# Two Strassen feed-forwards of a transformer block: modulation turns one place later, two loads earlier, a third set of sums and the last gates in another order

## The chip, the cores and the metric

The kernel runs on one core of one Trainium2 chip. The metric is the time of one execution on the device in microseconds (us). Before the change three runs gave 2195.95, 2199.52 and 2200.91 us; their median is 2199.52 us. Shares and times below are of the core's five engines: PE (TensorE, matmuls), DVE (VectorE), ACT (ScalarE), POOL (GpSimd) and SP (SyncE, which here only issues transfers).

## What is computed

One transformer block on 1024 latent tokens and 256 context tokens of width 1024, in float32. Both token sets pass a first feed-forward, then a token mixer (a bidirectional mLSTM beside banded attention), and the latent tokens pass a second feed-forward. Everything is modulated by vectors that come from a condition `c` through `w_ada`:

```python
mod_l = (jax.nn.silu(c) @ w_ada[l] + b_ada[l]).reshape(B, N_MOD, 1, D)      # nine vectors of 1024
def _ffn_sublayer(x, shift, scale, gate, w13, w2, g, b):
    h = x * (1.0 + scale) + shift
    a = h @ w13                                   # 1024 x 5632
    y = (silu(a[..., :2816]) * a[..., 2816:]) @ w2   # 2816 x 1024
    return _layer_norm(ALPHA * x + FFN_RES * gate * y, g, b)
```

## The kernel before

Each float32 operand is split into a rounded high part (ACT copies it) and a low part (DVE subtracts), and PE multiplies high by high, high by low and low by high. So every operand costs one ACT and one DVE instruction, and every 128-row tile three matmuls.

**First phases** (`quick1_*` for the first feed-forward F1, `quick2_*` for the second, F2). The products with `w13` run by Strassen's scheme in the form with seven products. There are 20 *starts* j, one for each block of 128 hidden columns beyond the first two. In a start PE runs seven products of 12 matmuls (`PRODUCTS`, i = 0 to 6), in F1 with four short products for the context rows between them. DVE adds products together (L1093: `u_sum`, twice `v_sum`, `x_c_sum`, `g_half`), makes the sums of the weights of the next start (L957 to L962) and their low parts (L990). PE's sixth product (i = 5) waits for the third of the L1093 sums, the second `v_sum`. The raw weights of the start after that are loaded when the low parts of `A12` and `A22` have been taken (`quick_weights`).

In F1's first phase DVE also works out the other seven modulation vectors. They come in 112 *slices* of `w_ada`, loaded one by one; DVE multiplies each into `ada_sums` (L741). For the first three vectors each slice is used twice, for latent and context. There are 20 such *units* (`MOD_UNITS`). When a unit is complete PE turns it by four small transposes (L757), and DVE reduces it and adds a bias (L766, L767). `mods_turned(j, place)` says in which of four places of a start a unit is turned. For PE the places are: before product i = 3, before i = 4, before i = 6, and before i = 1 of the next start. For DVE they are: after the low parts of S2 and S1, after the low part of S3, after the context gate (L1103), and after the first two low parts of the next start.

**Second phases** (`second1_*`, `last_*`). The products with `w2` run by Strassen too: seven products of 11 *pieces* each, 77 steps s, 12 matmuls each (L1483 to L1485). A piece is 128x1024: a half from the hidden rows, which the first phase has written to `f_terms`, and a half of `w2`. Six raw buffers (`RAWS`) hold pieces; ACT makes the high part (L1431), DVE the low part (L1470). The weights of products q = 1 to 4 are sums of two halves of `w2`, so another half, `s_kept`, is loaded for each of the 11 pairs, and DVE adds it to the raw piece (L1466). In step s DVE first does the sum of step s + 2 and then the low part of step s, in its own order.

SP issues everything in one queue in program order, and each issue waits for what frees its buffer. Pieces 0 to 3 are issued at the beginning of the last start, pieces 4 and 5 when the first phase's last product is done, and the others when the low part of the piece six before has been taken. The kept halves are issued one by one behind pieces 5 to 15, and each waits until the kept half two before it has landed:

```python
def kept_sp(sp, S, i):
    if i >= 2:
        sp.wait_ge(S.kept_in[i % 2], S.kept_before + 16 * (i // 2))
    sp.dma_start(S.kept[:, i], w2_view[...]).then_inc(S.kept_in[i % 2], 16)
```

The hidden rows of the last pair of blocks are also summed by DVE (`term_rest_dve`: L479, L481, L484) and stored by SP; the three sums come before the low part of piece 2.

**The end.** The last nine steps of the 77 (`TAIL`) run row tile by row tile: t = 0 goes through all nine pieces, then t = 1, 2 and 3. DVE multiplies each finished PSUM tile by the gate (L1540, `gate_part_dve`), adds it to the residual (L1549, `add_part_dve`), and norms the output rows (L3305, L3309, `out_rows_dve`). ACT takes the row sums of all rows but the last (`row_sums_act`), POOL the power (L3252). For the last row DVE does the statistics itself (L3286 to L3293).

## Time and profile before

| | |
|---|---|
| three runs | 2195.95, 2199.52, 2200.91 us |
| span of the profiled execution, first to last instruction | 2195.6 us |
| own time of the profiled execution | not given beside its span; the span is 0.35 us under the shortest run and 3.9 us under the median |
| PE busy | 2152.4 us, 98% |
| DVE busy | 1518.4 us, 69% |
| ACT busy | 890.3 us, 41% |
| DMA, mean over the span | 141 GB/s |
| F1: first phase with `quick1`, second phase | about 109 to 625 us, 625 to 900 us |
| F2: first phase with `quick2`, second phase | about 1590 to 1970 us, 1970 to 2185 us |

A matmul of 512 columns is shown as 0.39 us long, but in an unbroken run one starts every 0.2265 us, so the records overlap; a gap between records is therefore shorter than the time that PE lost. What is lost is read from the distances between starts. Three matmuls of one row tile take 0.68 us, one step of 12 takes 2.72 us.

### The profile page before, as it was taken

How to read it: one execution, taken by the hardware profiler on the slowest of the kernel's cores; microseconds unless marked ns; L12 is line 12 of the kernel's file. 1: busy time of each engine (PE TensorE's matmuls, PEld its weight loads, DVE VectorE, ACT ScalarE, POOL GpSimd, SP SyncE). 2: the span in 40 equal slices, each digit the busy share in tenths (PEclk: the TensorE clock that was granted, in tenths of full speed). 3: DMA queues.
4: the chain of work that ended last, by engine and by line, in shares of the span. 5: the costliest groups of instructions: out<-in, count | busy, mean ns of one | idle time of the engine just before them, and what ended most of it. 6: DMA issues, size and time to landing. Idle time of an engine off the chain costs nothing.

```text
span 2195.6 us, 32184 instructions
## 1 busy us (share of the span) xinstructions
PE 2152.4 (98%) x11779; PEld 1830.0 (83%) x11779; DVE 1518.4 (69%) x2595; ACT 890.3 (41%) x1502; POOL 161.0 (7%) x201
## 2 busy tenths in 40 slices
PE   9999999999999999999999999999999999999997
PEld 6888888888888888899789978888778888887886
DVE  5788887777548977755752356766767777767787
ACT  3622222222236455532543337733523333326444
POOL 0000000000000010370000004511000000000000
PEclk9999999999999999999999999999999999999999
DMA  8154444555269665532330003342233434439772
GB/s 289 32 156 143 144 141 135 164 164 172 78 232 317 202 187 170 163 125 61 108 99 21 20 1 110 108 130 77 72 130 109 153 119 146 126 122 323 270 234 100
DMA packets 261843, 310.41 MB, mean 141 GB/s; under 512 B 19350, under 2 KB 164686, under 8 KB 261710
## 3 DMA queue, kind: packets, MB, share of 16 engines
q1 hardware_dynamic: 250670, 300.13, 42.7%
q10 hardware_dynamic: 11040, 8.52, 1.3%
q8 instruction: 82, 1.34, 0.3%
q14 instruction: 51, 0.42, 0.1%
HBM read 242.13 MB, written 66.45 MB: 141 GB/s over the span
## 4 chain that ended last, share of the span: by engine, by line
PE 80%; DVE 9%; ACT 4%; DMA 4%; issue 3%; SPq 1%; POOL 0%; ACTq 0%; DVEq 0%; POOLq 0%
PE psum L1288 10%; PE psum L1290 10%; PE psum L1289 10%; PE psum L1483 5%; PE psum L1484 5%; PE psum L1485 5%; PE psum L1986 2%; PE psum L1988 2%; PE psum L1987 2%; PE psum L2407 2%; DMA raw<-in_ffn_w 2%; PE psum L1308 1%; PE psum L1307 1%; PE psum L1306 1%; DMA s_kept<-in_ffn_w 1%
## 5 line engine op out<-in xcount | busy, mean ns | idle before, releaser
L1288 PE MATMUL psum<-x_mix_h,x_op_h 128*128 128x512 f32 x640 | 251.0, 392 | 4.5 <-DVE v_sum L1093 4.5
L1289 PE MATMUL psum<-x_mix_l,x_op_h 128*128 128x512 f32 x640 | 249.5, 390 | 0.0
L1290 PE MATMUL psum<-x_mix_h,x_op_l 128*128 128x512 f32 x640 | 249.3, 390 | 0.0
L1483 PE MATMUL psum<-s_high 128*128 128x512 f32 x616 | 240.6, 391 | 4.4 <-DVE s_low L1470 4.2
L1484 PE MATMUL psum<-s_low,s_high 128*128 128x512 f32 x616 | 239.8, 389 | 0.0
L1485 PE MATMUL psum<-s_high,s_low 128*128 128x512 f32 x616 | 239.7, 389 | 0.0
L1470 DVE TENSOR_TENSOR s_low<-s_raw,s_high 128x1024 fp32r<-128x1024 f32 x154 | 187.2, 1217 | 52.9 <-ACT s_high L1431 52.9
L1431 ACT ACTIVATE s_high<-s_raw 128x1024 fp32r<-128x1024 f32 x154 | 161.7, 1057 | 128.9 <-PE psum L1485 56.2
L984 ACT ACTIVATE x_op_h<-raw 128x512 fp32r<-128x512 f32 x140 | 85.9, 627 | 212.1 <-PE psum L1290 131.2
L984 ACT ACTIVATE x_op_h<-w_sum 128x512 fp32r<-128x512 f32 x160 | 97.4, 626 | 160.6 <-DVE w_sum L962 103.6
L1288 PEld LDWEIGHTS psum<-x_mix_h,x_op_h 128*128 128x128 f32 x640 | 120.3, 188 | 29.3 <-DVE x_op_l L990 3.1
L1483 PEld LDWEIGHTS psum<-s_high 128*128 128x128 f32 x616 | 115.6, 188 | 31.6 <-DVE s_low L1470 7.8
L1290 PEld LDWEIGHTS psum<-x_mix_h,x_op_l 128*128 128x128 f32 x640 | 120.2, 188 | 25.5
L1289 PEld LDWEIGHTS psum<-x_mix_l,x_op_h 128*128 128x128 f32 x640 | 120.3, 188 | 23.5
L1485 PEld LDWEIGHTS psum<-s_high,s_low 128*128 128x128 f32 x616 | 115.6, 188 | 24.2
L1484 PEld LDWEIGHTS psum<-s_low,s_high 128*128 128x128 f32 x616 | 115.6, 188 | 23.8
L990 DVE TENSOR_TENSOR x_op_l<-raw,x_op_h 128x512 fp32r<-128x512 f32 x140 | 92.7, 685 | 35.8 <-ACT x_op_h L984 33.7
L1986 PE MATMUL psum<-p_wh,xh_lat 128*128 128x256 f32 x384 | 113.0, 294 | 0.0
L1988 PE MATMUL psum<-p_wh,xl_lat 128*128 128x256 f32 x384 | 108.8, 283 | 0.0
L1987 PE MATMUL psum<-p_wl,xh_lat 128*128 128x256 f32 x384 | 108.7, 283 | 0.0
L990 DVE TENSOR_TENSOR x_op_l<-w_sum,x_op_h 128x512 fp32r<-128x512 f32 x160 | 107.4, 683 | 0.1
L741 DVE SCALAR_TENSOR_TENSOR ada_sums<-ada_slice,more,ada_sums 128x512 f32<-128x512 f32 x140 | 99.6, 746 | 4.0 <-DVE ada_sums L746 0.5
(405 smaller groups left out, 5144.7 us busy)
## 6 DMA issues: line engine op xcount, KB each, us to landing
raw<-in_ffn_w SPq DMA_DIRECT2D x88, 512.0 KB, 5.4
f_terms<-g_half SPq DMA_DIRECT2D x154, 256.0 KB, 2.3
s_raw<-f_terms SPq DMA_DIRECT2D x154, 256.0 KB, 3.3
s_raw<-in_ffn_w SPq DMA_DIRECT2D x154, 256.0 KB, 4.2
ada_slice<-in_w_ada SPq DMA_DIRECT2D x112, 256.0 KB, 3.1
c_raw<-in_ffn_w SPq DMA_DIRECT2D x22, 512.0 KB, 3.8
p_raw<-in_w_in SPq DMA_DIRECT2D x22, 512.0 KB, 4.9
early<-in_w_ada SPq DMA_DIRECT2D x16, 512.0 KB, 6.4
```

The lines of the kernel that those rows point to most:

```text
L984: nc.scalar.activation(op_tiles(F, op)[0][:], OP_SOURCE[op], ACT.Copy).then_inc(F.hi, 1)
L990: nc.vector.tensor_tensor(low[:], OP_SOURCE[op], high[:].bitcast(F32), ALU.subtract).then_inc(F.lo, 1)
L1288: nc.tensor.matmul(o, wh[:, k], high(k), start=i < 4 and k == 0, stop=False, skip_group_check=i > 3)
L1289: nc.tensor.matmul(o, wh[:, k], low(k), start=False, stop=False, skip_group_check=i > 3)
L1290: last = nc.tensor.matmul(o, wl[:, k], high(k), start=False, stop=k == KH - 1, skip_group_check=i > 3)
L1431: nc.scalar.activation(S.high[s % RING][:], S.raw[s % RAWS][:], ACT.Copy).then_inc(F.hi, 1)
L1470: nc.vector.tensor_tensor(S.low[s % RING][:], S.raw[s % RAWS][:], S.high[s % RING][:].bitcast(F32), ALU.subtract)\
L1483: nc.tensor.matmul(o, h[:, 0, rows], h[:, 1], start=i == 0 and q in (0, 1, 6), stop=False, skip_group_check=True)
L1484: nc.tensor.matmul(o, h[:, 0, rows], l[:, 1], start=False, stop=False, skip_group_check=True)
L1485: return nc.tensor.matmul(o, l[:, 0, rows], h[:, 1], start=False, stop=i == PAIRS - 1, skip_group_check=True)
L1986: nc.tensor.matmul(o[:, 0:w], high, high_w[:, k, :], start=k == 0, stop=False)
L1988: last = nc.tensor.matmul(o[:, 0:w], low, high_w[:, k, :], start=False, stop=k == KD - 1)
```

## The change

Four edits, all in the two feed-forwards:

- Every unit of the modulation is turned one place later, on PE and on DVE.
- Pieces 4 and 5 of both second phases are issued within the last start of the first phase, before the last stores of the hidden rows. In F1 they wait for the last context product, in F2 for the third product of the last start. For that F2's raw buffers 4 and 5 move to another place in SBUF and change places with a ring buffer.
- The kept halves use four semaphores in place of two, so each waits only for the one four before it, and they are issued behind pieces 6 to 16.
- The sums of the last pair (`term_rest_dve`) come behind the low part of piece 2. At the end of F2 the four gates of `which = 2` come behind the last low part in place of among the last ones, and the output rows n = 6 are normed before the last gate instead of behind it.

```diff
-                    if SLICES[s] == (g, h, KD - 1) and 4 * i + q // 2 + v == at]
+                    if SLICES[s] == (g, h, KD - 1) and 4 * i + q // 2 + v + 1 == at]
...
                 ctx_store(sp, F, j + 2)
+                if j == QUICK - 1:
+                    for s in range(4, RAWS):
+                        pieces_sp(sp, S1, s)
...
                     term_sp(sp, F, p + 1, "S3")
+                    if last:
+                        for s in range(4, RAWS):
+                            pieces_sp(sp, S2, s)
                     term_sp(sp, F, p + 1, "A12")
...
-            term_rest_dve(dve, F, PAIRS - 1)
...
+            elif s < RAWS and F.n == 3:
+                sp.wait_ge(ctx_ready, 2 * QUICK)
             elif s < RAWS:
-                sp.wait_ge(F.ab_ready, F.products)
+                sp.wait_ge(F.ab_ready, F.products - 4)
...
         def kept_sp(sp, S, i):
-            if i >= 2:
-                sp.wait_ge(S.kept_in[i % 2], S.kept_before + 16 * (i // 2))
+            if i >= 4:
+                sp.wait_ge(kept_in[i % 4], kept_loaded(S, i) - 16)
...
-            for s in range(4, STEPS2):
+            for s in range(RAWS, STEPS2):
                 pieces_sp(sp, S, s)
-                if 5 <= s < 5 + PAIRS:
-                    kept_sp(sp, S, s - 5)
+                if RAWS <= s < RAWS + PAIRS:
+                    kept_sp(sp, S, s - RAWS)
...
                 pieces_low(dve, S, s)
+                if s == 2:
+                    term_rest_dve(dve, F, PAIRS - 1)
...
-                if 74 <= s < 76:
-                    for t in range(2 * s - 148, 2 * s - 146):
-                        gate_part_dve(dve, S, 2, t)
+            for t in range(4):
+                gate_part_dve(dve, S, 2, t)
             for t in range(4):
                 add_part_dve(dve, S, 2, t)
             for t in range(4):
+                if t == 3:
+                    out_rows_dve(dve, 6)
                 gate_part_dve(dve, S, 3, t)
                 add_part_dve(dve, S, 3, t)
-                if t:
+                if 0 < t < 3:
                     out_rows_dve(dve, 4 + t - 1)
                 if t == 2:
                     half_sums_dve(dve, 3, 1)
+            dve.wait_ge(F.y_added, 40)
             half_sums_dve(dve, 3, 0)
```

What it does to the order, at three places. First SP around the end of F1's first phase, before (`s_raw_291` and `s_raw_292` are the raw buffers of pieces 4 and 5, `s_raw_287` and `s_raw_288` those of pieces 6 and 7):

```order
L440 DMA f_rows<-g_ctx 128x256
L460 DMA f_terms<-g_half_157 128x512
L460 DMA f_terms<-g_half_155 128x512
L460 DMA f_terms<-g_half_154 128x512
L460 DMA f_terms<-g_half_156 128x512
L1392 DMA s_raw_291<-f_terms 128x512
L1394 DMA s_raw_291<-in_ffn_w 128x512
L1392 DMA s_raw_292<-f_terms 128x512
L1394 DMA s_raw_292<-in_ffn_w 128x512
L1400 DMA s_kept<-in_ffn_w 128x512
L1392 DMA s_raw_287<-f_terms 128x512
```

and in the changed kernel, whose lines are numbered a little differently:

```order
L441 DMA f_rows<-g_ctx 128x256
L1398 DMA s_raw_291<-f_terms 128x512
L1400 DMA s_raw_291<-in_ffn_w 128x512
L1398 DMA s_raw_292<-f_terms 128x512
L1400 DMA s_raw_292<-in_ffn_w 128x512
L461 DMA f_terms<-g_half_157 128x512
L461 DMA f_terms<-g_half_155 128x512
L461 DMA f_terms<-g_half_154 128x512
L461 DMA f_terms<-g_half_156 128x512
L1398 DMA s_raw_287<-f_terms 128x512
L1400 DMA s_raw_287<-in_ffn_w 128x512
L1406 DMA s_kept<-in_ffn_w 128x512
```

Pieces 4 and 5 have moved ahead of the four last stores, and the first kept half has moved behind piece 6.

Second DVE at the end of F2, from the last but two low parts to the last gates, before:

```order
L1470 TENSOR_TENSOR s_low_333<-s_raw_318,s_high_324 128x1024
L1540 TENSOR_TENSOR s_sums<-psum,gate_row_276 128x512 x2
L1470 TENSOR_TENSOR s_low_334<-s_raw_319,s_high_325 128x1024
L1540 TENSOR_TENSOR s_sums<-psum,gate_row_276 128x512 x2
L1470 TENSOR_TENSOR s_low_335<-s_raw_320,s_high_326 128x1024
L1549 SCALAR_TENSOR_TENSOR y<-y,s_sums 128x512 x4
```

and in the changed kernel:

```order
L1480 TENSOR_TENSOR s_low_333<-s_raw_318,s_high_324 128x1024
L1480 TENSOR_TENSOR s_low_334<-s_raw_319,s_high_325 128x1024
L1480 TENSOR_TENSOR s_low_335<-s_raw_320,s_high_326 128x1024
L1550 TENSOR_TENSOR s_sums<-psum,gate_row_276 128x512 x4
L1559 SCALAR_TENSOR_TENSOR y<-y,s_sums 128x512 x4
```

The last two low parts no longer stand behind two gates each.

Third DVE in start 2 of F1's first phase, where a unit is turned; before:

```order
L1093 TENSOR_TENSOR v_sum<-psum,v_sum 128x512
L990 TENSOR_TENSOR x_op_l_114<-w_sum,x_op_h_106 128x512
L766 TENSOR_REDUCE ada_sum<-psum 128x4
L767 TENSOR_TENSOR mod<-ada_sum,params 128x4
L1093 TENSOR_TENSOR x_c_sum<-psum,u_sum 128x512
L1098 TENSOR_TENSOR g_half_154<-g_half_154,x_c_sum 128x512
L1103 TENSOR_TENSOR g_ctx<-psum,g_ctx 128x256
L766 TENSOR_REDUCE ada_sum<-psum 128x4
L767 TENSOR_TENSOR mod<-ada_sum,params 128x4
L990 TENSOR_TENSOR x_op_l_115<-raw,x_op_h_107 128x512
```

and in the changed kernel:

```order
L1100 TENSOR_TENSOR v_sum<-psum,v_sum 128x512
L991 TENSOR_TENSOR x_op_l_114<-w_sum,x_op_h_106 128x512
L1100 TENSOR_TENSOR x_c_sum<-psum,u_sum 128x512
L1105 TENSOR_TENSOR g_half_154<-g_half_154,x_c_sum 128x512
L1110 TENSOR_TENSOR g_ctx<-psum,g_ctx 128x256
L767 TENSOR_REDUCE ada_sum<-psum 128x4
L768 TENSOR_TENSOR mod<-ada_sum,params 128x4
L991 TENSOR_TENSOR x_op_l_115<-raw,x_op_h_107 128x512
```

The latent unit has moved behind the context gate, and the context unit from there into the next start, ahead of that start's second group of slices. PE's transposes have moved likewise.

## Rows read from the trace of the kernel before

**Rows 1.** The page, part 1: busy time, share of the span, instructions of each engine.

```profile
PE 2152.4 (98%) x11779; PEld 1830.0 (83%) x11779; DVE 1518.4 (69%) x2595; ACT 890.3 (41%) x1502; POOL 161.0 (7%) x201
```

**Rows 2.** Waits of PE, whole span: us in total, times, longest.

```profile
PE psum L1288 <- DVE v_sum L1093: 4.5, 4, 1.8
...
PE psum L757 <- DVE ada_sums L741: 2.5, 3, 1.3
```

**Rows 3.** The page, part 5, second phases: busy, mean ns, idle before, what ended it.

```profile
L1483 PE MATMUL psum<-s_high 128*128 128x512 f32 x616 | 240.6, 391 | 4.4 <-DVE s_low L1470 4.2
```

**Rows 4.** Waits of PE in 620 to 660, 1950 to 2010, 2010 to 2196 us.

```profile
PE psum L1483 <- DVE s_low L1470: 0.8, 2, 0.4
...
PE psum L1483 <- DVE s_low L1470: 1.6, 2, 1.5
...
PE psum L1483 <- DVE s_low L1470: 1.8, 2, 1.4
```

**Rows 5.** Timeline of PE, F1's starts 7 and 8: start us, us, operation, idle before.

```profile
290.88 0.39 PE L1288 MATMUL psum<-x1h,x_op_h 128*128 128x512 f32 x1
...
316.71 0.39 PE L1288 MATMUL psum<-x1h,x_op_h 128*128 128x512 f32 x1
...
331.98 0.63 PE L757 MATMUL psum<-ident,ada_sums 128*128 128x128 f32 x4 [1.32 <-DVE ada_sums L741]
...
336.63 0.40 PE L1288 MATMUL psum<-x_mix_h,x_op_h 128*128 128x512 f32 x1
...
344.01 0.39 PE L1288 MATMUL psum<-x1h,x_op_h 128*128 128x512 f32 x1
```

**Rows 6.** Timeline of DVE in start 8 of F1.

```profile
324.63 0.69 DVE L957 TENSOR_TENSOR w_sum<-raw 128x512 f32<-128x512 f32 x1 [0.29 <-issue]
...
333.55 0.68 DVE L1093 TENSOR_TENSOR v_sum<-psum,v_sum 128x512 f32<-128x512 f32 x1
...
339.58 0.69 DVE L1093 TENSOR_TENSOR x_c_sum<-psum,u_sum 128x512 f32<-128x512 f32 x1 [3.95 <-PE psum L1290]
```

**Rows 7.** Waits of SP, 1960 to 2040 us.

```profile
SPq L1400 <- DMA s_kept<-in_ffn_w: 9.5, 9, 2.2
```

**Rows 8.** Timelines of DVE, SP and ACT, F2's change of phase.

```profile
1974.71 2.35 DVE L1470 TENSOR_TENSOR s_low<-s_raw,s_high 128x1024 fp32r<-128x1024 f32 x2
...
1995.38 0.69 DVE L1466 TENSOR_TENSOR s_raw<-s_raw,s_kept 128x512 f32<-128x512 f32 x1 [4.61 <-DMA s_kept<-in_ffn_w]
...
1975.25 0.40 SPq L1392 DMA_DIRECT2D s_raw<-f_terms  x1
...
1979.53 1.06 ACT L1431 ACTIVATE s_high<-s_raw 128x1024 fp32r<-128x1024 f32 x1 [5.61 <-DMA s_raw<-in_ffn_w]
```

**Rows 9.** Timeline of PE, F2's second phase: steps 0 and 9.

```profile
1970.30 0.39 PE L1483 MATMUL psum<-s_high 128*128 128x512 f32 x1
...
1997.26 0.50 PE L1483 MATMUL psum<-s_high 128*128 128x512 f32 x1 [1.47 <-DVE s_low L1470]
...
1998.06 0.40 PE L1483 MATMUL psum<-s_high 128*128 128x512 f32 x1
```

**Rows 10.** Stretches: PE, PEld, DVE, ACT, POOL busy, granted clock, DMA share, GB/s.

```profile
1975.00:1996.00 21.00, 20.53 (x88) 16.01 (x87) 8.81 (x9) 7.42 (x7) 0.00 (x0) 1.00 1.00 334
...
2166.00:2184.00 18.00, 18.00 (x81) 14.86 (x80) 11.65 (x15) 8.40 (x18) 1.62 (x3) 1.00 0.09 36
```

**Rows 11.** Timelines of DVE and POOL, the last 40 us.

```profile
2160.78 1.28 DVE L1540 TENSOR_TENSOR s_sums<-psum,gate_row 128x512 f32<-128x512 f32 x2
...
2182.73 0.69 DVE L3286 BATCH_NORM_STATS2 out_stats<-y 128x6 f32<-128x512 f32 x1
...
2185.05 0.69 DVE L1540 TENSOR_TENSOR s_sums<-psum,gate_row 128x512 f32<-128x512 f32 x1 [1.64 <-issue]
...
2188.90 0.69 DVE L3286 BATCH_NORM_STATS2 out_stats<-y 128x6 f32<-128x512 f32 x1
...
2183.30 0.54 POOL L3252 TENSOR_TENSOR out_stats<-out_stats,consts 128x1 f32<-128x1 f32 x1 [5.58 <-ACT out_stats L3282]
```

More of the change, by code:

```diff
@@ L284, in hybrid_block @@
         g_in = [sem(f"g_in{i}") for i in range(2)]
+        kept_in, loads_before_kept = x_in + g_in[:1], (4, 4, 2, 0)
         steps = [0]
@@ L1263, in quick2_dve @@
             body(TL + 1, 1, True, False)
-            term_rest_dve(dve, F, PAIRS - 1)
         def quick_product(pe, F, j, i, first):
@@ L1352, in hybrid_block, with __init__ @@
         class Second:
-            def __init__(self, F, name, raws, ring, ring_free, kept, parts, sums, x_bank, y_bank, before, loads_before, kept_in,
-                         kept_before):
+            def __init__(self, F, name, raws, ring, ring_free, kept, parts, sums, x_bank, y_bank, before, loads_before):
                 self.F = F
@@ L1366, in __init__ @@
                 self.ring_free = ring_free
-                self.loads_before, self.kept_in, self.kept_before = loads_before, kept_in, kept_before
+                self.loads_before, self.kept_before = loads_before, before
             def bank(self, q, t):
@@ L1397, in kept_sp, with kept_loaded @@
         def kept_sp(sp, S, i):
-            if i >= 2:
-                sp.wait_ge(S.kept_in[i % 2], S.kept_before + 16 * (i // 2))
-            sp.dma_start(S.kept[:, i], w2_view[S.F.which][2 * i * P:(2 * i + 1) * P, BANK:D]).then_inc(S.kept_in[i % 2], 16)
+            if i >= 4:
+                sp.wait_ge(kept_in[i % 4], kept_loaded(S, i) - 16)
+            sp.dma_start(S.kept[:, i], w2_view[S.F.which][2 * i * P:(2 * i + 1) * P, BANK:D]).then_inc(kept_in[i % 4], 16)
+        def kept_loaded(S, i):
+            return 16 * (loads_before_kept[i % 4] + S.kept_before * len(range(i % 4, PAIRS, 4)) + i // 4 + 1)
         def piece_in_place(engine, S, s):
@@ L1460, in pieces_sum @@
             if q == 1:
-                dve.wait_ge(S.kept_in[i % 2], S.kept_before + 16 * (i // 2 + 1))
+                dve.wait_ge(kept_in[i % 4], kept_loaded(S, i))
             else:
@@ L3216, in hybrid_block @@
         LAST_ROWS = list(range(4, TL)) + list(range(4))
-        G_BEFORE = (len(range(0, PAIRS, 2)), len(range(1, PAIRS, 2)))
+        G_BEFORE = (2 * len(range(3, PAIRS, 4)), 0)
         def x2_rows_dve(dve, p):
@@ L3226, in last_sp @@
         def last_sp(sp):
-            for s in range(4, STEPS2):
+            for s in range(RAWS, STEPS2):
                 pieces_sp(sp, S2, s)
-                if 5 <= s < 5 + PAIRS:
-                    kept_sp(sp, S2, s - 5)
+                if RAWS <= s < RAWS + PAIRS:
+                    kept_sp(sp, S2, s - RAWS)
                 if s % 2 and 27 <= s < 27 + 2 * TL:
@@ L3318, in last_dve @@
                 pieces_low(dve, S, s)
+                if s == 2:
+                    term_rest_dve(dve, F, PAIRS - 1)
                 if s == 29:
@@ L3380, in hybrid_block @@
         S1 = Second(F1, "s1", (120, 124, 196, 200, 72, 76), (144, 0, 8, 160, 168, 176, 184, 16, 24), ring_free1,
-                    32, (112, 136, 152), 54, 4, 0, 0, loads1, g_in, 0)
-        S2 = Second(F2, "s2", (120, 124, 196, 200, 32, 36), (156, 164, 172, 180, 0, 72, 148, 112, 128), ring_free2,
-                    8, (40, 48, 56), 64, 4, 0, 1, loads2, raw_in, 16 * (F2.raws_before + FB))
+                    32, (112, 136, 152), 54, 4, 0, 0, loads1)
+        S2 = Second(F2, "s2", (120, 124, 196, 200, 72, 76), (156, 164, 172, 180, 0, 32, 148, 112, 128), ring_free2,
+                    8, (40, 48, 56), 64, 4, 0, 1, loads2)
         block = keep.enter_context(nc.Block())
```

## The prediction, made before the changed kernel ran

> **What bounds the kernel.** I read the page's shares first: PE is busy 98% of the span [rows 1], so only time in which PE waits can be won, apart from what follows PE's last matmul. The second view is the list of PE's waits. Three of its groups lie where the change edits: the wait of a modulation turn for `ada_sums`, 2.5 us in three times, the waits of the second phases for a low part, 4.2 us in six times, 4.4 with two short ones, and the waits for `v_sum`, 4.5 us in four times [rows 2, 3]. The list by stretch puts the second group at three places: the beginning of each second phase and F2's end [rows 4]. The third view is the timeline around each wait, for what DVE did before it. The fourth is DMA: full at F2's change of phase, share 1.00 at 334 GB/s [rows 10].
>
> A gap between records is not what PE loses. A matmul is shown as 0.39 us long while one starts every 0.2265 us, so 0.16 more is lost, and after a wait the first three take 0.80 us in place of 0.68 [rows 9]. Each wait of the second phases thus costs its gap plus 0.28 us. For the turns I take the distance between starts: 27.30 us with a gap of 1.32, 25.83 in the start before, with two turns as well [rows 5]; 1.47 lost, the gap plus 0.15.
>
> **Turns one place later.** What ends the three waits is DVE's slice work just ahead of the turn; a place later DVE is past it. The gaps sum to 2.5 us [rows 2], with 3 x 0.15 they cost 2.9. No operation is added; the four transposes and DVE's two instructions move; these I put at 0.85 us, from the 0.69 us of a 128x512 instruction [rows 6] and a bias add on four columns. What is late next is the third L1093 sum, for which product i = 5 waits. In start 8 it ends at 334.23 [rows 6] and the product starts at 336.63 [rows 5], 2.40 later. Without the stall (1.47) and with the four transposes (0.39, an estimate from three matmuls' usual spacing around them) behind that product rather than ahead, the product wants to start at 334.77. The turned unit also comes ahead of `A12` and `A22`'s low parts in starts 1, 4 and 7. That delays the next raw weights by about 0.85 - 0.39 = 0.47 us, and start 8 was already waiting 0.29 us before its weight sums [rows 6]. So the sum ends at 334.70: 0.07 us of room. Starts 3, 6 and 9 get 0.85 us more on DVE ahead of that sum and 0.46 on PE. Starts 10 to 17 keep their unit ahead of it. Bounds: nothing given back, or in starts 2, 3, 5, 6, 8 and 9 each 0.85 + 0.15, 6.0 in all, more than is won. I take 0.3 given back, near the measured room. Term: 2.6 us, from -3.1 to +2.9.
>
> **Pieces 4 and 5 earlier, four semaphores, sums behind piece 2.** In F1 PE waits 0.8 us in two steps and in F2 1.6 in two [rows 4]; the other 0.2 of the page's 4.4 [rows 3] are one short gap of 0.1 in each. With 0.28 for each of three waits F1 loses 0.9 + 0.8 = 1.7 us and F2 1.7 + 0.8, with the rounding 2.6. The waits are at steps 2, 4 and 9. Step 2: its low part stands behind the three sums, and comes 2.0 us earlier. Step 4: the piece landed 4.3 us after its issue at 1975.25 and ACT began at 1979.53 [rows 8]; now it is in place before the phase begins. Step 9: DVE does the sum of piece 11 first, and that had to wait till 1995.38 [rows 8]; the low part follows, 1.93 us with the sum. From step 0 at 1970.30 [rows 9] step 9 is due nine steps of 2.72 us later, at 1994.75, so piece 11 has to be there at 1992.8.
>
> When will it be? Before, 8 pieces and 6 kept halves, 22 transfers of 262 KB or 5.77 MB, went from 1975.25 to 1995.38; less 1.7 us for the first to arrive that is 313 GB/s, with SP waiting 9.5 us for kept halves [rows 7]. Now piece 6 is issued behind the last store. Low part 2 began at 1974.71 behind three sums of 0.69, about 2.0 us, and a low part takes 1.2 [rows 8]: the gate before them had ended at 1972.7, and now come the low part, the sums and two more issues of SP, to 1976.7. Six pieces and the five kept halves between them are 17 transfers, 4.46 MB, 14.2 us at 313 GB/s: 1992.6, by 0.2 us in time. At the 334 GB/s of the stretch [rows 10] it is 1991.8. F1 has 0.9 us of room at its own rate of 330. After that a step needs 786 KB each 2.72 us, 289 GB/s, so the lead grows. The sums before step 3's low part leave it 1.1 us. The loads' issue in the first phase costs nothing: SP has no other work there, DVE and PE don't wait for it, and the stores behind need the gate of 1972.7 first. If this cover is gone, the four issues (0.4 us each by the row of 1975.25 [rows 8]) make the stores and piece 6 about 1.7 us late. Bounds for both phases: all 4.3 us won, or step 9 keeps its waits (0.7 and 1.75), 1.9 won; an added loss of 1.0 if more loads in flight each land later. I take 4.0: near the upper end, since both step 9s come out in time at the rates of the rows.
>
> **F2's end.** Four gates, two before each of the last two low parts, take 1.28 us a pair [rows 11]; PE waited twice, 1.8 us [rows 4], with 0.56 that is 2.4 lost. Without the gates the last two low parts start where the first pair of gates did, at 2160.78 [rows 11], and are ready at 2162.0 and 2163.2. PE's last tile was ready at 2185.05 [rows 11]; 84 matmuls of 0.2265 us, 0.16 and the 0.12 of a fresh start before that it began the last piece, at 2165.7, and without the 2.4 us it wants that piece at 2163.3 and the one before at 2162.6: no wait left, and no other work on DVE is late, for the first PSUM tile of the last product needs DVE only after the gates and adds (about 2168, as before). Bounds 1.4 to 2.4; I take 2.4.
>
> The order of the last rows: from the last gate at 2185.05 to the last statistics at 2188.90 it takes 3.85 us [rows 11], of which the norm of row 6 is 2.5. It moves ahead of the gate. It can't begin before DVE's statistics end at 2183.42 (2182.73 + 0.69) and takes till 2185.97; POOL's power, ready at 2183.84 [rows 11], is in time for its second instruction. So the last gate starts 0.9 us late and 1.6 are won, less 0.1 for the added wait on the add. Term 1.5, bounds 0.5 and 2.5.
>
> **What the clock adds.** The granted clock is 1.00 in the stretch with F2's longest wait and in the one that follows the last wait [rows 10], the level of 2.4 GHz, and PE's matmuls have their usual spacing again 0.80 us after it [rows 9]; a removed wait returns its own length and no more. The Trainium skill, page "TensorE: Matmul & The Clock Gate", section "HAM oscillation — how this bites in real kernels", says that waits of PE in the middle of work can throw the array back to half clock. By that rule the longest wait would also have made matmuls behind it start every 0.45 us, some 6 us for a block of 27, and the gain here would be about 17 us in place of 10.5. The rows hold against it, so it gets no share of the sum.
>
> **Sum.** 2.6 + 4.0 + 2.4 + 1.5 = 10.5 us, 0.5%. The span of the profile is 2195.6 us and becomes 2185.1. The median of the three runs lies 3.9 us above that span, for which no row shows a place, so I take the difference off the median: 2199.5 - 10.5 = 2189.0 us.
>
> **Rivals.** (a) The transfers stay the bound. For it speaks a DMA share of 1.00 [rows 10] and the 0.2 us of room in F2; and four kept halves in flight share the same bandwidth with the pieces. Then step 9 keeps its waits, 2.3 us less than the 4.0 taken, and the turns give back 1.5 in place of 0.3: 10.5 - 2.3 - 1.2 = 7.0, 2192.5 us. Against it speaks that 1 MB less is to be carried in the full stretch.
>
> (b) DVE is the real bound of F1's first phase, and the wait only moves from the turn to product i = 5, as the four `v_sum` waits [rows 2] show that it can; all 2.9 come back, the step 9 waits stay, and the late rows of the end give only 0.5. Then 10.5 - 2.6 - 2.3 - 1.0 = 4.6, 2194.9 us, hardly to be told from no change. Against it: 0.07 to 2 us of room by the trace in each start.
>
> (c) Slower: the raw weights. A turned unit that stands ahead of the low parts of `A12` and `A22`, or in the next start's beginning, makes each later load of raw weights 0.85 us later; if DVE had no idle time to absorb this, every one of the 17 starts that follow a slice would be 0.85 longer, 14.5 us, and 10.5 - 14.5 gives 2203.5 us. It decides from about 0.6 us per start. Against it: DVE waits 3.95 us for PE in the middle of start 8, the tightest of them, before the sum at 339.58 [rows 6], so a delay ahead of it is not handed on.
>
> (d) The change does not do what it says, as where the last store's wait blocks SP: piece 6 would come later than piece 4 did by more than the 3 us that two pieces take. Then F2 and F1 keep all their waits and the gain is 2.6 + 2.4 + 1.5 = 6.5, 2193.0 us. It is 1.45 us later by the rows, so I count it with (a).
>
> **Chances.** Forecast (8.5 to 13 us won) 0.62, (a) with (d) 0.22, (b) 0.11, (c) 0.05. A measurement of this kernel can tell about 0.2%, 4.4 us, from no change. Faster by more: the forecast, nearly all of (a), a little of (b): 0.85. Within it 0.11, slower 0.04. The range: the forecast's own is 2186.5 to 2191; the lowest run before, 2195.95, less 12 gives 2184 as the lower end, and (a) and half of (b) on a median 2 us too high give 2196.
>
> **What would show it.** Turns: no wait of L757, and the starts 2, 5 and 8 within 0.3 us of 25.8; a new wait of L1288 for `v_sum` in start 8 or 5 would be the give-back. Second phases: raw pieces 4 and 5 issued before the stores, ACT's high parts of pieces 2 to 5 back to back, steps 2, 4 and 9 of both without a wait. A wait at step 9 of F2 alone means that the transfers bound it. End: no wait for a low part, and from the last gate to the last statistics 1.4 us in place of 3.85, the gate itself 0.9 after PE's last tile. The prediction is wrong if PE's waits in the two feed-forwards still sum to over 5 us, or if one of the other stages, which the change doesn't touch, takes over 1 us longer or shorter.

## The result and the profile after

Four runs of the changed kernel gave 2184.74, 2184.93, 2185.09 and 2185.97 us, median 2185.01; four of the kernel before had a median of 2199.20. The ratio is 0.9924, with a 95% interval of 0.991 to 0.9939: 16.7 us less, 13.4 to 19.8. The two medians differ by 14.2 us, which lies in that interval too. A second comparison, with 6 and 29 runs, gave 0.9923 (0.9905 to 0.9941), with medians 16.0 us apart. The forecast was 10.5 us less and 2189.0 us; the time lies 4 us below it, and below the forecast's own range of 2186.5 to 2191, though inside the outer range of 2184 to 2196. The gain is above the forecast even at the lower end of its interval.

The profiled execution has a span of 2183.3 us and a time of its own of 2185.09, so 1.8 us lie outside the span. Before, the span was 2195.6; with the same 1.8 us that execution took 2197.4, 3.6 us less than the kernel before usually takes (85 runs: 2194.75 to 2211.20, median 2201.0). Cut at the places that the prediction speaks of (a stage begins with its first matmul), the two spans differ so:

| us | before | after | difference | predicted |
|---|---|---|---|---|
| up to F1's first product with `quick1` | 109.41 | 108.09 | -1.32 | 0 |
| F1's first phase | 515.81 | 512.49 | -3.32 | -2.6 |
| F1's second phase | 210.64 | 208.81 | -1.83 | -1.7 |
| token mixer | 748.58 | 749.40 | +0.82 | 0 |
| F2's first phase | 385.86 | 385.70 | -0.16 | 0 |
| F2's second phase | 213.82 | 208.79 | -5.03 | -2.3 and -2.4 |
| from the last row tile's last three matmuls on | 11.48 | 10.02 | -1.46 | -1.5 |

The page's first part, and from its fifth the line of the second phases:

```profile
PE 2147.8 (98%) x11775; PEld 1830.7 (84%) x11779; DVE 1518.7 (70%) x2595; ACT 889.6 (41%) x1502; POOL 160.8 (7%) x201
...
L1493 PE MATMUL psum<-s_high 128*128 128x512 f32 x616 | 239.6, 389 | 0.0
```

The 4.4 us of idle time ahead of the second phases' matmuls [rows 3] are gone entirely. From the list of PE's waits over the whole span:

```profile
PE psum L1293 <- DVE v_sum L1100: 4.0, 3, 1.7
```

It has no turn wait, which in [rows 2] was 2.5 us in three times; the waits for `v_sum` are 4.0 us in place of 4.5. PE in starts 7 and 8 of F1, which answers to [rows 5] (start us, us, operation; the third row is product i = 5, the others are beginnings of a start):

```profile
287.68 0.39 PE L1293 MATMUL psum<-x1h,x_op_h 128*128 128x512 f32 x1
...
313.45 0.39 PE L1293 MATMUL psum<-x1h,x_op_h 128*128 128x512 f32 x1
...
331.39 0.40 PE L1293 MATMUL psum<-x_mix_h,x_op_h 128*128 128x512 f32 x1
...
338.77 0.39 PE L1293 MATMUL psum<-x1h,x_op_h 128*128 128x512 f32 x1
```

Start 8 takes 25.32 us in place of 27.30, start 7 25.77 in place of 25.83. DVE in start 8, which answers to [rows 6]: the third sum, and the unit in its new place behind the context gate:

```profile
330.04 0.68 DVE L1100 TENSOR_TENSOR v_sum<-psum,v_sum 128x512 f32<-128x512 f32 x1
...
336.20 0.69 DVE L767 TENSOR_REDUCE ada_sum<-psum 128x4 f32<-128x512 f32 x1
```

The sum ends at 330.72, 0.67 us before the product that waits for it; 0.07 was predicted.

F2's change of phase. SP, ACT, DVE and PE, which answer to [rows 8, 9]; step 0 is the first PE row, step 9 the second:

```profile
1954.71 0.38 SPq L1398 DMA_DIRECT2D s_raw<-f_terms  x1
...
1970.81 0.39 SPq L1398 DMA_DIRECT2D s_raw<-f_terms  x1
...
1966.12 3.89 ACT L1441 ACTIVATE s_high<-s_raw 128x1024 fp32r<-128x1024 f32 x4
...
1986.60 0.69 DVE L1476 TENSOR_TENSOR s_raw<-s_raw,s_kept 128x512 f32<-128x512 f32 x1 [3.76 <-DMA s_raw<-in_ffn_w]
1987.21 1.22 DVE L1480 TENSOR_TENSOR s_low<-s_raw,s_high 128x1024 fp32r<-128x1024 f32 x1
...
1964.49 0.39 PE L1493 MATMUL psum<-s_high 128*128 128x512 f32 x1
...
1988.97 0.39 PE L1493 MATMUL psum<-s_high 128*128 128x512 f32 x1
```

Piece 5 is issued at 1954.71, before the stores, and piece 6 at 1970.81, behind them. The high parts of pieces 2 to 5 stand back to back. Step 9 comes 24.48 us after step 0, nine steps of 2.72, so without a wait. Its low part ended at 1988.43, half a microsecond in time. The transfers still fill the queues, as in [rows 10]:

```profile
1969.00:1986.00 17.00, 17.00 (x76) 14.08 (x75) 8.40 (x9) 6.32 (x7) 0.00 (x0) 1.00 0.97 336
```

SP's waits for a kept half from 1960 to 2040, 9.5 us in [rows 7]:

```profile
SPq L1406 <- DMA s_kept<-in_ffn_w: 0.5, 1, 0.5
```

And DVE's last 10 us, which answer to [rows 11]: the norm of row 6, the last gate and the last statistics.

```profile
2172.62 1.29 DVE L3317 SCALAR_TENSOR_TENSOR y<-y,out_stats,ln_rows 128x1024 f32<-128x1024 f32 x1
2173.94 1.28 DVE L3321 SCALAR_TENSOR_TENSOR y<-y,out_stats,ln_rows 128x1024 f32<-128x1024 f32 x1
2175.14 0.68 DVE L1550 TENSOR_TENSOR s_sums<-psum,gate_row 128x512 f32<-128x512 f32 x1
2175.86 0.69 DVE L1559 SCALAR_TENSOR_TENSOR y<-y,s_sums 128x512 f32<-128x512 f32 x1
2176.58 0.69 DVE L3298 BATCH_NORM_STATS2 out_stats<-y 128x6 f32<-128x512 f32 x1
```

From the last gate to the last statistics it takes 1.44 us in place of 3.85.

So every term came out in the profile about as large as predicted: 11.6 us in the four stages that the terms name, against 10.5. What was too small is what these waits cost in the *other* executions of the kernel before. The experiments show two parts of that. A third, that the median of the kernel before lies above its profiled execution, is argued from them.

### The profile page after: what moved, and what is told of

Its sections match the earlier page's. It is cut to its first block, busy times and chain, and to the rows that moved or that the text cites. A ratio compares the mean times of both kernels' runs of the same rounds, so it can differ in the third digit from the quotient of the medians.

```text
span 2183.3 us, 32181 instructions
## 1 busy us (share of the span) xinstructions
PE 2147.8 (98%) x11775; PEld 1830.7 (84%) x11779; DVE 1518.7 (70%) x2595; ACT 889.6 (41%) x1502; POOL 160.8 (7%) x201
## 4 chain that ended last, share of the span: by engine, by line
PE 87%; DVE 7%; ACT 3%; issue 2%; DMA 1%; SPq 0%; POOL 0%; ACTq 0%; DVEq 0%; POOLq 0%
PE psum L1293 11%; PE psum L1294 11%; PE psum L1295 11%; PE psum L1493 6%; PE psum L1495 6%; PE psum L1494 6%; PE psum L1998 2%; PE psum L2000 2%; PE psum L1999 2%; PE psum L2419 2%; PE psum L1313 2%; PE psum L1312 2%; PE psum L1311 2%; PE psum L2973 1%; PE psum L2402 1%
```

## The experiments

Each kernel ran in 6 to 12 timed executions beside 17 to 35 of the kernel before on the same chip; the times of one kernel spread by 4 to 16 us, so the 95% interval of such a ratio reaches 0.1 to 0.2% to each side. What a stage lost is read in its profile from the distances between starts, against 208.8 us for a second phase without a wait. Apart from the unchanged kernel, the kernels cut from the one before (turns, end, sums, gates, and the two early pieces) count the kept halves on another pair of semaphores than it does; this was not tried alone. Theory A is the prediction's: each wait has its place and its price, as the one profile has them. Theory B is that a part wins more than that profile shows.

**The kernel before once more**, its text unchanged.

> The kernel before, once more, unchanged. Its runs spread over 5 us (2195.95 to 2200.91), those of the changed kernel over 1.2 us. Theory A (the change gives back the removed waits and nothing else; the rest of the measured difference is what this kernel's runs differ among themselves): ratio 1.000, and its profile may differ from the first one by 1 to 3 us in stretches that no edit touches, the first 100 us above all. Theory B (some runs of before wait longer at the places that the change edits, so that it takes off more than one profile shows): this second profile has waits at step 9 of the second phases, or of the modulation turns, that differ by 0.5 us or more from 0.43, 1.47 and 2.5 us.

2201.12 us (2197.39 to 2205.78), ratio 1.0002 (0.9989 to 1.0015). The same code lost 3.6 us in F1's second phase where the first profile had lost 1.8, and 4.6 in F2's (5.0 before). Its span was 2198.1. So theory B's sign is there: the waits at the edited places differ from one execution of the same text to the next.

**The turns alone.**

```diff
-                    if SLICES[s] == (g, h, KD - 1) and 4 * i + q // 2 + v == at]
+                    if SLICES[s] == (g, h, KD - 1) and 4 * i + q // 2 + v + 1 == at]
```

> The kernel before with the modulation's turns one place later, and nothing else. Theory A: first phase of F1 shorter by 3.3 us as in the changed kernel (515.8 to 512.5 us from the first product to the second phase), all else equal: about 2195.9 us against 2199.2. Rival (the wait moves to product i = 5): 0 to 1 us won. Theory B: 4 us or more.

2197.69 us, ratio 0.9990 (0.9979 to 1.0002), 2.2 us less, which the interval doesn't tell from no change. The turn waits are gone and no new one of their length has come. F1's first phase took 512.89 us. Over all profiles of this study it took 516.8 us on average in eight kernels with the turns at their old place (514.6 to 519.5) and 513.0 in five with the new one (512.5 to 513.6; the last kernel below, which changes start 0 too, is left out): 3.8 us for a term of 2.6. Of these, 0.2 lie in start 0, which the edit leaves alone.

**The change of phase alone**: pieces 4 and 5, the four semaphores and the place of the three sums; turns and end as before.

```diff
+                    if last:
+                        for s in range(4, RAWS):
+                            pieces_sp(sp, S2, s)
...
-            if i >= 2:
+            if i >= 4:
...
+                if s == 2:
+                    term_rest_dve(dve, F, PAIRS - 1)
```

> The kernel before with the edits at both changes of phase: pieces 4 and 5 earlier, four semaphores, sums behind piece 2; turns and end as before. Theory A: 1.8 us in F1 and 2.6 in F2, 4.4 us: 2194.8 us. Theory B: the loads in the full stretch vary from run to run, so this edit takes 6 to 9 us off the median and its runs lie closer together than those of before.

2193.55 us (2192.64 to 2196.70), ratio 0.9974 (0.9966 to 0.9983): 5.7 us less, 3.7 to 7.5. No wait is left in steps 0 to 12 of either phase. A's 4.4 lies inside the interval, towards its end, and so does the lower end of B's 6 to 9; the medians differ by 6.9. The times don't decide between the two. In this profile the clock was at 0.50 behind the wait of 1.37 us at F2's end, where the edit does nothing, and that end lost 3.9 us in place of 2.4.

**The end alone**: the four gates behind the last low part, and row 6 ahead of the last gate.

```diff
-                if 74 <= s < 76:
-                    for t in range(2 * s - 148, 2 * s - 146):
-                        gate_part_dve(dve, S, 2, t)
+            for t in range(4):
+                gate_part_dve(dve, S, 2, t)
...
+                if t == 3:
+                    out_rows_dve(dve, 6)
```

> The kernel before with F2's end as changed: four gates behind the last low part, row 6 normed before the last gate. Theory A: 2.4 us from the gates and 1.5 from the rows, 3.9 us: 2195.3 us. Rival (the two overlap, for a later gate eats what an earlier PE wins): 2.4 to 3 us.

2197.40 us, ratio 0.9990 (0.9980 to 1.0001). Both parts of the term are in the profile: the steps behind the change of phase lost nothing in place of 2.4, and the last stage took 10.01 in place of 11.48. The time, 2.2 us less by the ratio, can't be told from no change. The span was 2197.0, longer than that of the first profile. The largest part of the reason is at step 9 of F1, which has nothing to do with the end:

```profile
655.23 0.50 PE L1487 MATMUL psum<-s_high 128*128 128x512 f32 x1 [1.82 <-DVE s_low L1474]
655.57 0.40 PE L1488 MATMUL psum<-s_low,s_high 128*128 128x512 f32 x1
655.80 0.45 PE L1489 MATMUL psum<-s_high,s_low 128*128 128x512 f32 x1
656.05 0.63 PE L1487 MATMUL psum<-s_high 128*128 128x512 f32 x1
...
657.33 0.63 PE L1487 MATMUL psum<-s_high 128*128 128x512 f32 x1
658.61 0.63 PE L1487 MATMUL psum<-s_high 128*128 128x512 f32 x1
...
659.67 0.39 PE L1487 MATMUL psum<-s_high 128*128 128x512 f32 x1
```

Behind the wait of 1.82 us three matmuls take 1.28 us in place of 0.68, and the stretches before, in and behind it show the granted clock (third number from the right):

```profile
650.00:653.40 3.40, 3.40 (x16) 2.48 (x14) 0.05 (x1) 1.06 (x1) 0.00 (x0) 1.00 0.83 283
655.90:659.30 3.40, 3.40 (x10) 2.66 (x9) 2.97 (x4) 2.48 (x4) 0.00 (x0) 0.51 1.01 376
659.60:665.00 5.40, 5.40 (x26) 4.47 (x25) 4.02 (x5) 3.54 (x5) 0.00 (x0) 1.00 0.97 328
```

After the wait the array ran at 1.2 GHz, half of full speed, for eight matmuls, and lost 1.6 us more (0.60, 0.60 and 0.38, read from the distances, against 0.68); then it was back at 2.4 GHz. Here F1's change of phase lost 4.8 us where the first profile had lost 1.8.

**The whole change** once more, its text unchanged.

> The changed kernel again, for more runs of it. Single edits gave 2.7 (turns), 6.9 (changes of phase) and 3.0 us (end) off the median. If they add up: 12.6 us off, 2187.8 us for a before of 2200.4; if the spread of before comes mostly from the places that are edited, its runs lie within 2 us of each other but for the first 110 us. Rival: more than the sum, 15 us or more off, because a shift in one place also takes a wait away in another.

2186.28 us (2182.44 to 2187.69), ratio 0.9923 (0.9905 to 0.9941). The span was 2183.7, and the stages are within 1.1 us of those of the table above; no wait in steps 0 to 12. By the ratios this is 16.9 us less, and the three parts alone come to 2.2, 5.7 and 2.2, 10.1 in all (by the medians 16.0 and 12.6). That is the size which the rival of more than the sum asked for. The intervals of the whole and of the three together reach some 4 us to each side, and no stage of the profiles wins clearly more in the whole than in its part, so it stays open whether the 6.8 us between the two are more than noise.

**Pieces 4 and 5 alone**: issued in the last start as in the whole change, with the kept halves one piece later.

```diff
-            for s in range(4, STEPS2):
+            for s in range(RAWS, STEPS2):
                 pieces_sp(sp, S, s)
-                if 5 <= s < 5 + PAIRS:
-                    kept_sp(sp, S, s - 5)
+                if RAWS <= s < RAWS + PAIRS:
+                    kept_sp(sp, S, s - RAWS)
```

> The kernel before with pieces 4 and 5 issued in the first phase, kept halves behind pieces 6 to 16, still on two semaphores, sums still ahead of piece 2's low part. If the bytes in the full stretch decide (2 pieces, 1.05 MB, 3 us at 340 GB/s): the waits at steps 4 and 9 go in both phases, 0.4 us of step 2 stay in each: 6 us of the 6.9 off, 2194.4 us. If it is the number of loads in flight: step 9 keeps most of its 1.8 us, and less than 3.5 us are won.

2195.50 us, ratio 0.9971 (0.9959 to 0.9982), 6.4 us less. The waits of steps 4 and 9 are gone in both phases, with two semaphores and with the sums ahead; each phase lost 0.4 us, at step 2. This edit alone does the transfers' part. In this profile the clock was at 0.50 after the wait of 1.36 us at F2's end, and that phase lost 3.9 us there in place of 2.4. Around it, with the clock in the same place of the line:

```profile
2160.00:2163.30 3.30, 1.52 (x6) 0.62 (x4) 3.30 (x5) 0.00 (x0) 0.00 (x0) 1.00 0.00 0
2163.90:2166.80 2.90, 2.90 (x8) 2.21 (x8) 2.76 (x5) 0.00 (x0) 0.00 (x0) 0.50 0.00 0
```

Behind the same wait the first profile has a clock of 1.00 [rows 10].

**Four semaphores alone.**

```diff
-            if i >= 2:
-                sp.wait_ge(S.kept_in[i % 2], S.kept_before + 16 * (i // 2))
+            if i >= 4:
+                sp.wait_ge(kept_in[i % 4], kept_loaded(S, i) - 16)
```

> The kernel before with the kept halves on four semaphores, in their old places, and nothing else. If SP's waits for kept halves (9.5 us in nine waits) hold back the pieces: piece 11 is issued 3 to 5 us earlier and the wait at step 9 falls by 1 us or more in each phase, 2 to 4 us off. If the transfers are the bound: issued earlier but landed at the same time, under 1 us off, 2200 us.

2198.50 us, ratio 0.9986 (0.9974 to 0.9998), 3.1 us less, 0.4 to 5.7. Steps 4 and 9 still wait: 1.9 us lost in F1 and 1.9 in F2, where the five profiles with the old code lost 3.2 on average in each, but between 1.8 and 5.0 singly. So one profile doesn't show that the semaphores shorten these waits. Here the turn of start 8 waited 1.92 us, and the clock was at 0.50 from 333.8 on; F1's first phase took 519.5 us, the longest of all.

**The place of the sums alone.**

```diff
-            term_rest_dve(dve, F, PAIRS - 1)
...
+                if s == 2:
+                    term_rest_dve(dve, F, PAIRS - 1)
```

> The kernel before with the sums of the last pair behind piece 2's low part, and nothing else. The wait at step 2 goes (0.37 us in each phase, 0.7 in all); but the last stores, and the pieces 4 and 5 behind them, are issued 1.2 us later, so if the transfers bound the stretch, steps 4 and 9 wait 1.2 us longer each in total: between 0.7 us won and 1.7 us lost.

2204.23 us, ratio 1.0003 (0.9987 to 1.0019). Step 2's wait goes, but as the stores and all pieces behind them come later, steps 4 and 9 wait longer: the changes of phase lost 7.6 and 6.7 us, with 1.6 of the 7.6 behind a drop of the clock. This execution took 2208.86 us, 4.6 more than the median of its kernel. PE's waits in F2's change of phase, with which 1.6 us in [rows 4] compares:

```profile
PE psum L1485 <- DVE s_low L1472: 5.6, 3, 3.2
```

Alone this edit doesn't pay.

**The four gates alone**, without the new order of the last rows.

> Only the four gates at F2's end go behind the last low part; the last rows keep their order. Of the whole part at F2's end the run before won 3.0 us, of which 1.45 us lay behind PE's last matmul. Theory A (each term has its own place): no wait for a low part after 2140 us, F2's second phase 2.1 us shorter from its wait at the end alone, the stretch behind PE's last matmul still 11.5 us; 2.1 to 2.4 us won, within the noise of 2.5 us of such a run. Rival (the gates' time comes back at the end, since the adds start later): the stretch behind grows by over 1 us and nothing is won.

2198.87 us, ratio 0.9980 (0.9968 to 0.9993), by the ratio 4.4 us less (1.5 to 7.0). The steps behind the change of phase lost nothing in place of 2.4, so 2.4 won, and the last stage took 11.50 as before: theory A. In F2's change of phase, again outside the edit, step 9 waited 2.44 us, and the clock fell behind it:

```profile
1999.67 0.50 PE L1487 MATMUL psum<-s_high 128*128 128x512 f32 x1 [2.44 <-DVE s_low L1474]
...
2001.71 0.63 PE L1487 MATMUL psum<-s_high 128*128 128x512 f32 x1
```

The stretches around it, with the clock third from the right:

```profile
1996.00:2000.40 4.40, 1.96 (x9) 1.34 (x8) 2.43 (x3) 2.12 (x3) 0.00 (x0) 1.00 1.03 381
2000.50:2003.90 3.40, 3.40 (x10) 2.63 (x9) 2.96 (x3) 2.68 (x4) 0.00 (x0) 0.50 1.00 348
2004.10:2010.00 5.90, 5.90 (x27) 4.88 (x26) 4.80 (x6) 3.80 (x6) 0.00 (x0) 1.00 1.02 366
```

That phase change lost 5.0 us, against 2.6 in the first profile.

**The whole change with two semaphores.**

> The whole change without the four semaphores: two as before, so SP waits for each kept half before it issues the next but one. Theory A (bytes in the full stretch decide, as with the two pieces alone): no wait of PE in steps 0 to 12 of either phase, the waits of SP for a kept half back at 7 to 10 us, and 15 to 16 us won as with the whole change. Rival (loads must stand close behind one another): steps 4 or 9 wait again for 0.5 us or more in each phase, and 12 to 14 us are won.

2188.21 us, ratio 0.9935 (0.9917 to 0.9954). No wait of PE in steps 0 to 12, while SP waits for kept halves as it did in [rows 7]:

```profile
SPq L1406 <- DMA s_kept<-in_ffn_w: 8.9, 9, 1.3
```

That is theory A: SP's wait alone costs nothing once the pieces are early. This profiled execution was longer than its kernel's median, at 2196.3 us, mostly through one wait in the token mixer, which no edit touches:

```profile
PE psum L1998 <- DVE p_wl L1945: 6.7, 1, 6.7
```

DVE's two subtractions ahead of it took 16.57 us together, where all twenty of them in the profile of the whole change took 1.2 to 1.8 us each. The clock was at 0.50 from 962.3 to 969.1, which began while PE waited, and again from 972.6 to 976.0. The token mixer took 760.3 us in all, against 747.1 to 751.4 in the thirteen other profiles. No run shows why DVE was slow here.

**The whole change with the sums ahead of the low parts.**

> The whole change with the three sums of the last pair ahead of the second phase's low parts, as before. Theory A (the sums' place decides the wait at step 2 alone, since pieces 4 and 5 no longer stand behind the stores): step 2's wait of about 0.4 us is back in both phases and costs 0.7 us in each as distance between steps at most, steps 4 and 9 have none; 14 to 15.5 us won. Rival (the sums also decide when the next raw pieces come): step 9 waits again in F2, and under 13 us are won.

2186.43 us, ratio 0.9933 (0.9913 to 0.9953). Each second phase loses 0.4 us at step 2 and nothing at 4 and 9, as with pieces 4 and 5 alone. The intervals of this kernel, of the one with two semaphores and of the whole change overlap, so the times don't tell them apart.

**The whole change, and start 0's slices later.** Product i = 5 of start 0 waits 1.65 us for the third sum, the longest wait left in F1.

```diff
-                slices(j, 1)
+                if j:
+                    slices(j, 1)
...
+                if not j:
+                    slices(j, 1)
                 slices(j, 2)
```

> The whole change, and in start 0 of F1 the four slices of its second place come behind the third sum and the low part after it, since product i = 5 of start 0 waits 1.65 us for that sum, and 2.7 us of slices stand ahead of it. Theory A (the wait is DVE's order alone): the wait of start 0 goes, F1's first phase is 1.65 + 0.15 = 1.8 us shorter than with the whole change, and the time is 1.8 us below it, which is less than such a run can tell; the profile shows it. Rival (the four slices then stand ahead of the sum for the ring, and release their buffers later): PE waits in start 0 or 1 for another product, and the phase is not shorter by 1 us.

2189.03 us, ratio 0.9935 (0.9915 to 0.9955): not better than the whole change, and F1's first phase took 515.79 us where the whole change had 512.5 and 513.6. The rival was right. The wait of start 0 is gone and a longer one stands in start 1, with the clock down behind it:

```profile
156.04 0.47 PE L1296 MATMUL psum<-x_mix_h,x_op_h 128*128 128x512 f32 x1 [2.86 <-DVE v_sum L1100]
...
157.10 0.63 PE L1296 MATMUL psum<-x_mix_h,x_op_h 128*128 128x512 f32 x1
```

DVE had these slices' 2.7 us to do in any case, and then waited for the next slices to arrive:

```profile
132.75 2.74 DVE L742 SCALAR_TENSOR_TENSOR ada_sums<-ada_slice,more,ada_sums 128x512 f32<-128x512 f32 x4 [2.07 <-DMA ada_slice<-in_w_ada]
```

## Why the prediction was right in kind and too small in size

Two steps of it failed. The term of 4.0 us for the changes of phase was sized from one profile, and these waits cost 6.4 us on average over five. And "a removed wait returns its own length and no more" doesn't hold: in other executions the clock fell behind such waits. The stages named, their waits and their order of events came out as forecast.

**The turns.** Right: the three waits are gone, nothing is given back. Predicted 2.6, in the profile 3.3, on average over the profiles 3.8. The give-back of 0.3 did not come, because start 8's sum ended 0.67 us in time. In starts 10 to 13 the sum ends 0.18 to 0.62 us ahead of its product, and in start 14 the product waits 0.13 us, the only new wait. So rival (b) is out. So is rival (c): no start from 1 to 17 takes over 25.8 us. The sign given for starts 2, 5 and 8, 25.8 us within 0.3, was missed: they take 25.32 each, because the unit's transposes have moved into the next start, and starts 3, 6 and 9 take 25.32 in place of 24.86.

**The changes of phase: the term that was mis-sized.** Right in mechanism: steps 2, 4 and 9 lose their waits in both phases, piece 11 came 15.8 us after piece 6's issue, 316 GB/s by the prediction's own reckoning, where it took 313. Rival (a), transfers that stay the bound, is refuted by seven kernels with early pieces, none of which loses over 0.2 us at steps 4 and 9. The size was taken from one profile. In the five profiles with the old order of loads (before, again, turns, end, gates) F1's change of phase lost 1.8, 3.6, 3.4, 4.8 and 2.2 us and F2's 2.6, 2.2, 2.9, 3.5 and 5.0: 3.2 and 3.2 on average, 6.4 together, where the term was 4.0 of 4.3. Of these 6.4, 0.6 are two drops of the clock. The first two profiles alone, which are of the kernel before itself, give 5.1; the other three have the other pair of semaphores. The waits at steps 4 and 9 end with a transfer at a DMA share of 1.00, and their length changes from one execution to the next. Why it does is not shown by any run here.

**F2's end and the last rows.** Right: 2.4 and 1.46 us, predicted 2.4 and 1.5. DVE's own order of instructions sets these waits, and they had the same length in all seven profiles with the old order of gates (1.36 or 1.37 us for the longer one). The cost was 2.4 us in four of them and 3.9 or 4.0 in the three that had a drop of the clock behind the wait, 3.1 on average.

**What the clock adds: the step that was wrong in kind.** The prediction said that "a removed wait returns its own length and no more", because the clock stayed at 1.00 around the longest wait of one profile, and gave the rule of the Trainium skill (page "TensorE: Matmul & The Clock Gate", section "HAM oscillation — how this bites in real kernels") no share. The other profiles show clock drops behind such waits. Over 14 profiles PE waited 1.3 us or longer in the two feed-forwards 51 times, and behind 9 of these waits the clock was at 0.50 for some eight matmuls: behind a turn, behind waits for `v_sum`, at step 9 of F1 and of F2, and at F2's end. It isn't the length of the wait alone that decides: the same wait of 1.36 us at F2's end had a drop behind it in 3 profiles of 7, and the longest of the 51, 3.19 us, had none. What does decide is not shown. Each drop costs 1.5 to 1.6 us beyond the wait. At 9 in 51, and some three or four such waits that the change removes, that is 0.8 to 1.1 us per execution. By that rule such a wait takes the clock down each time that it comes; the section has it for waits of about 3 to 5 us that come back with every tile. Here it was one wait in six, and 8 of the 9 were shorter than 3 us, so the runs agree only in that a wait can do it; what a drop costs is a quarter of the 6 us that the prediction made of it.

The timed runs fit this from the other side, though they show only that the two go together. Each has its span and its mean granted clock. In 81 runs of the kernel before the mean clock was 0.9945; the 31 at 0.994 had a mean span of 2200.7 us, the 3 at 0.997 one of 2193.8, the 2 at 0.992 one of 2208.0. With the whole change (10 runs) the mean is 0.9962. Span times the missing share is 12.2 us before and 8.3 after. Of these 3.9 us 1.5 are the end, where PE has no work (4.1 us missing in the first profile, 2.6 in the changed kernel's). The other 2.4 are more than the drops of the last paragraph explain, which at 1.7 of this measure each come to 0.9 to 1.2. Ahead of F1's first product this measure was 5.1 us or more in six of nine profiles without the whole change and in two of five with it, and 3.4 in the others, which gives another 0.6 on average. No edit touches that part of the program, so this may be chance. The rest isn't settled.

**The sum again.** With means over profiles in place of the one: 3.8 for the turns, 3.1 for F1's second phase, 6.3 for F2's (3.2 at its beginning and 3.1 at its end, drops counted in both) and 1.5 for the last rows make 14.7 us, inside the measured 13.4 to 19.8 and 2 us below its middle. The prediction noted that the median lies 3.9 us above the span and that no row shows where. 1.8 of these are outside any span. The other 2.1 are of the size of what the edited places lose on average beyond the first profile (2.0 in the changes of phase, 0.7 at F2's end), so they belonged into the gain, and into the range above all; no row of the timed runs themselves shows it.

**The prediction's own signs of being wrong.** Both were there, by a little. From `quick1` on PE's waits in the two feed-forwards still sum to 5.1 us, where it said 5; all of them are waits for `v_sum` and for the low part ahead of F2's first product, which the edits leave alone. And the stretch before F1's first product, which no edit touches, was 1.3 us shorter, where it said 1; over all profiles that stretch took 107.8 to 112.3 us, so 1.3 us are within what it varies by.

**What the experiments say about the parts.** Pieces 4 and 5 carry the transfers' part by themselves. The later sums add 0.4 us per phase at step 2, and nothing can be shown for the four semaphores beside the early pieces. Without the early pieces the later sums won nothing in the timed runs.

## What to carry to other kernels

A wait that a transfer ends is a sample: one profile shows one length of it, here stages with such waits lost 1.8 to 5.0 us with the same loads in the same order, so its removal is worth the mean over several profiles, while a wait that an engine's own order makes (1.36 us at F2's end) has the same length in each. If the profiled execution is faster than the median, take a second profile before the sum, and look whether the rest is in such waits; if it is, it counts to the gain of a change that removes them. And a removed wait of PE can be worth more than its length: count the chance of a stretch at 1.2 GHz behind it (here 9 in 51, 1.6 us each).

## What the runs showed that was not expected

- Short drops of TensorE's clock, from 2.4 to 1.2 GHz for some eight 512-column matmuls (0.43 us apart in place of 0.2265), behind waits of 1.36 to 3.0 us, in 9 of 51 cases, at places where the same wait had none in other executions.
- With all queues full (share 0.97 to 1.03) the DMA moved 328 to 336 GB/s in some stretches of the change of phase, 376 and 381 in others, and 399 in the 17 us from 661 us on in the first profile, at a share of 1.04; why is not explained. So the 313 GB/s that the prediction reckoned with was no ceiling.
- A fix for one late sum (start 0) made a later and longer wait of 2.86 us in start 1: the slices' 2.7 us of DVE were only moved, and behind them DVE waited 2.07 us for the next slices.
- Two DVE subtractions in the token mixer took 16.57 us together in one execution, where each takes 1.2 to 1.8 in another; PE waited 6.7 us for them. No run shows the cause.
